# A two-block layer in f32r halves: head rows spread by one f32r matmul of two rows, embedding projection by split weights, rotary products in another order

## What is computed

```python
# first block
h = h + 0.5 * swiglu(rmsnorm(h, norm_ffn1), ffn1_w1, ffn1_w3, ffn1_w2)
z = rmsnorm(h, norm_mix) @ w_in
q, kc, vc, ksl, vsl, kw, vw, g, u = split(z)
q, kc, ksl, kw = rope(q), rope(kc), rope(ksl), rope(kw)     # x1*cos - x2*sin, x1*sin + x2*cos
o_nsa = nsa_attention(q, kc, vc, ksl, vsl, kw, vw, sigmoid(g), ...)
o_s5 = s5_mixer(u, ...)
h = h + concatenate([o_nsa, o_s5]) @ w_out
h = h + 0.5 * swiglu(rmsnorm(h, norm_ffn2), ffn2_w1, ffn2_w3, ffn2_w2)
h = h + sigmoid(rmsnorm(h, norm_ple) @ w_ple_gate) * (p @ w_ple)   # p: 512 x 256
h = rmsnorm(h, norm_final)
# second block, twice: projections, recurrence, and per head of the cell (4 heads of 256)
d = b[t] - b[s] + log_i[s]          # s <= t, b the running sum of log_f
m_t = max(m_inter, max(d)); w_intra = exp(d - m_t)
num = (q k^T * w_intra) v + ...; den = sum(q k^T * w_intra) + ...
h = num / max(|den|, exp(-m_t))
```

## Time and profile before

| | |
|---|---|
| median of 3 runs | 2105.43 us (2105.28 to 2106.63) |
| the profiled execution | 2098.56 us, its span 2096.8 us |
| TensorE busy | 1996.2 us, 95% of the span |
| VectorE, ScalarE, GpSimd busy | 1228.6, 844.0, 362.4 us |
| mean granted TensorE clock | 0.965 of full speed |

### The profile page before, as it was taken

One profiled execution on the slowest core, in us unless ns is written; L12 is line 12 of the kernel. 1 busy time (PEld: TensorE's weight loads), 2 busy tenths in 40 slices (PEclk: granted clock), 3 DMA queues, 4 the chain that ended last, 5 costly groups with the idle time before them and its releaser, 6 DMA issues.

```text
span 2096.8 us, 21907 instructions
## 1 busy us (share of the span) xinstructions
PE 1996.2 (95%) x8662; PEld 1526.7 (73%) x8662; DVE 1228.6 (59%) x1636; ACT 844.0 (40%) x1264; POOL 362.4 (17%) x319
## 2 busy tenths in 40 slices
PE   7999999988977899999999999999999899999997
PEld 5888888756533478888887777776788778766886
DVE  5764444677696446665665686924662559335742
ACT  5331323201456543322333347644542366445531
POOL 2000001156244010000001302601201024102002
PEclk9999999998778999999999999999999999999998
DMA  5332232221000134654652222321123222220221
GB/s 185 100 118 75 100 104 97 84 71 53 26 0 1 65 131 158 208 182 158 198 173 68 71 91 78 101 81 51 51 91 100 83 86 81 91 70 31 91 90 61
DMA packets 53174, 196.70 MB, mean 94 GB/s; under 512 B 5969, under 2 KB 6481, under 8 KB 52433
## 3 DMA queue, kind: packets, MB, share of 16 engines
q1 hardware_dynamic: 42912, 159.50, 22.7%
q0 software_dynamic: 7504, 28.58, 4.3%
q10 hardware_dynamic: 2656, 7.23, 1.0%
HBM read 192.14 MB, written 2.10 MB: 93 GB/s over the span
## 4 chain that ended last, share of the span: by engine, by line
PE 78%; DVE 13%; ACT 4%; POOL 2%; issue 1%; DMA 1%; ACTq 0%; POOLq 0%; DVEq 0%
PE PS L554 77%; DVE AR L1546 3%; DVE AR L1779 2%; DVE WLO L1543 2%; ACT WHI L1078 1%; DVE AR L2021 1%; DVE AR L1869 1%; PE PS L768 1%; DVE AR L1988 0%; DMA H<-in_xT 0%; POOL ACC L2137 0%; DVE ACC L1546 0%; DMA RAW<-in_w_out 0%; ACT SQ L1093 0%; DVE AR L1759 0%
## 5 line engine op out<-in xcount | busy, mean ns | idle before, releaser
L554 PE MATMUL PS<-HNH,WHI 128*128 128x512 f32 x1632 | 658.7, 404 | 15.8 <-ACT HNH L1109 13.9
L1543 DVE TENSOR_TENSOR WLO<-RAW,WHI 128x1024 fp32r<-128x1024 f32 (+1 forms) x270 | 371.6, 1379 | 514.7 <-ACT WHI L1078 514.5
L554 PE MATMUL PS<-HNH,WLO 128*128 128x512 f32 x1632 | 639.8, 392 | 3.4 <-DVE WLO L1543 3.4
L1078 ACT ACTIVATE WHI<-RAW 128x1024 fp32r<-128x1024 f32 (+1 forms) x270 | 295.9, 1096 | 687.0 <-PE PS L554 613.3
L554 PE MATMUL PS<-HNL,WHI 128*128 128x512 f32 x1632 | 436.0, 390 | 0.1
L554 PEld LDWEIGHTS PS<-HNH,WHI 128*128 128x128 f32 x1632 | 308.2, 189 | 96.4 <-issue 22.0
L554 PEld LDWEIGHTS PS<-HNH,WLO 128*128 128x128 f32 x1632 | 308.5, 189 | 77.9 <-issue 8.9
L554 PEld LDWEIGHTS PS<-HNL,WHI 128*128 128x128 f32 x1632 | 307.4, 188 | 64.8 <-DVE HNL L1546 1.0
L554 PE MATMUL PS<-AR 128*128 128x512 f32 (+12 forms) x700 | 213.3, 519 | 8.7 <-DVE SQ L1763 3.6
L2137 POOL TENSOR_TENSOR ACC<-ACC,SQ 128x512 f32<-128x512 f32 x46 | 62.7, 1362 | 782.2 <-ACT SQ L1093 781.3
L554 PEld LDWEIGHTS PS<-AR 128*128 128x128 f32 (+5 forms) x700 | 99.4, 199 | 90.2 <-issue 57.6
(11 more groups left out here) (299 smaller groups left out, 2421.6 us busy)
## 6 DMA issues: line engine op xcount, KB each, us to landing
RAW<-in_w_in SPq DMA_DIRECT2D x80, 512.0 KB, 3.5
AR<-in_w_ada POOLq DMA_DIRECT2D x48, 512.0 KB, 3.9
RAW<-in_w13a SPq DMA_DIRECT2D x44, 512.0 KB, 3.3
RAW<-in_w13b SPq DMA_DIRECT2D x44, 512.0 KB, 4.2
RAW<-in_w_out SPq DMA_DIRECT2D x40, 512.0 KB, 3.5
RAW<-in_w2a SPq DMA_DIRECT2D x16, 704.0 KB, 4.1
RAW<-in_w2b SPq DMA_DIRECT2D x16, 704.0 KB, 5.6
RAW<-in_w_inA SPq DMA_DIRECT2D x12, 512.0 KB, 3.3
```

Source lines behind the costliest of these rows:

```text
L554: return pe.matmul(o, l, r, start=start, stop=stop, skip_group_check=True)
L1078: act.activation(hi_of(name, i), raw_of(name, i), ACT.Copy).then_inc(*HI.up(name, i))
L1543: dve.tensor_tensor(lo_of(name, i), raw_of(name, i), f32(hi_of(name, i)), S_).then_inc(*LO.up(name, i))
```

## The change

- **Cell.** VectorE writes for each of NM and MM a pair of rows, a high row (rounded to f32r) at partition 32h and a low row at 32h + 1, with signs turned (`minus_rows`: one operation that writes the rounded row, one that forms both by the mask lo_row); sel_i and sel_f now put each head's gates on two partitions. TensorE opens a head with two f32r matmuls of two rows instead of two f32 matmuls of one. The ones that it multiplies with are copied once to f32r by ScalarE.
- **Embedding projection.** w_ple goes through the split stream as two tiles of 1024 columns, each for four output tiles, at m = 0 and m = 3; p is split once, ahead of the second feed-forward. ScalarE waits there for its load.
- **Rotary order.** GpSimd makes the cosine product in the step "rope". Turn 2 stands behind "positions" 0, the turns 4 and 5 come one step later, 6 and 7 within the value products.

The diff, with one line of context:

```diff
@@ -22,7 +22,7 @@
     ("norm_g", 16), ("b_ada", 48), ("rg_conv_w", 64), ("rg_conv_b", 16), ("rg_b_a", 16), ("rg_b_x", 16),
-    ("rg_lam", 16), ("ml_conv_w", 64), ("ml_conv_b", 16), ("ml_norm_g", 16), ("final_g", 8), ("b_if", 2),
+    ("rg_lam", 16), ("ml_conv_w", 64), ("ml_conv_b", 16), ("ml_norm_g", 16), ("final_g", 8), ("b_if", 2), ("lo_row", 1),
 ]
@@ -75,7 +75,9 @@
     ffn("b")
-    out.extend(("w_pg", m, 1024, True) for m in range(8))
+    for c, tiles in enumerate((range(3), range(3, 8))):
+        out.append(("w_ple", c, 1024, True))
+        out.extend(("w_pg", m, 1024, True) for m in tiles)
     for l in range(2):
@@ -223,19 +225,22 @@
             yield "pairs", 0
-        elif i > 2:
-            yield "turn", i - 1
         if i == 3:
...
             yield "pairs", 1
+        if i in (3, 4):
+            yield "turn", i - 1
+        if i > 5:
+            yield "turn", i - 2
         if i >= 4:
...
     yield "positions", 1
-    yield "turn", 7
     for z in range(2):
...
             yield "v", z, tt
+            if z == 0 and tt < 2:
+                yield "turn", 6 + tt
             yield from some(1)
@@ -336,6 +341,9 @@
         OH, OL = tiles_(place("OH", at_ar, 8 * T, F32R)), tiles_(place("OL", at_ar + 9216, 8 * T, F32R))
+        ROW_HALF = tiles_(place("ROW_HALF", at_ar + 4096 + T, T, F32R))[:, 0, :]
+        ROWS = tiles_(place("ROWS", at_ar + 4096 + 4 * T, 2 * T, F32R))
+        ONE = place("ONE", at_ar + 20640, P, F32R)
         MASK = place("MASK", at_ar + 20520, 2 * P, mybir.dt.bfloat16)
@@ -380,7 +388,7 @@
             loaded(f"x{k}")
-        for name in ("vecs", "consts", "s5_bc", "small_w", "pairs", "w_ple", "pT", "c", "rg_w", "w_if"):
+        for name in ("vecs", "consts", "s5_bc", "small_w", "pairs", "pT", "c", "rg_w", "w_if"):
             loaded(name)
@@ -491,8 +499,8 @@
 
-        WP = ar(0, 2, 1024)
         PT_ = ar(2048, 2, T)
+        PTH, PTL = tiles_(place("PTH", at_ar, 2 * T, F32R)), tiles_(place("PTL", at_ar + 2 * T, 2 * T, F32R))
         ACC2 = ar(3072, T)
@@ -826,18 +834,29 @@
 
+            ple_banks = {}
             for m in range(KD):
-                ps2, b2 = take(pe, "w_ple", m)
-                pe.wait_ge(*loaded("w_ple").at())
-                pe.wait_ge(*loaded("pT").at())
-                for k in range(2):
-                    t = mm(ps2[:, :], WP[:, k, P * m:P * m + P], PT_[:, k, :], k == 0, k == 1)
-                t.then_inc(*P_.up("w_ple", m))
+                if m in (0, 3):
+                    c = m // 3
+                    hi, lo = rows(hi_of("w_ple", c), T), rows(lo_of("w_ple", c), T)
+                    for j in range(4):
+                        w = slice(P * j, P * j + P)
+                        ple_banks[4 * c + j] = ps, b = take(pe, "ple", 4 * c + j)
+                        for k in range(2):
+                            pe.wait_ge(*HI.at("w_ple", c))
+                            pe.wait_ge(*A.at("pt", k))
+                            mm(ps[:, :], hi[:, k, w], PTH[:, k, :], k == 0, False)
+                            pe.wait_ge(*LO.at("w_ple", c))
+                            mm(ps[:, :], lo[:, k, w], PTH[:, k, :], False, False)
+                            pe.wait_ge(*V.at("pt", k))
+                            t = mm(ps[:, :], hi[:, k, w], PTL[:, k, :], False, k == 1)
+                        t.then_inc(*P_.up("ple", 4 * c + j))
+                    P_.name("w_ple", c)
                 b = tile("w_pg", m, HNHk, HNLk, hn("ple"))
...
                 give(b, V, "ple_in", m)
-                give(b2, V, "ple_out", m)
+                give(ple_banks[m][1], V, "ple_out", m)
             P_.name("ple_done")
@@ -1002,13 +1021,14 @@
                     if step == "open":
-                        r = slice(32 * h, 32 * h + 1)
+                        r = slice(32 * h, 32 * h + 2)
                         bm[h] = take(pe, "cell_m", l, h)
                         pe_, be = take(pe, "cell_e", l, h)
+                        pe.wait_ge(*A.at("one"))
                         pe.wait_ge(*V.at("nm", l))
-                        mm(bm[h][0][:, :], const("ones")[r, :], NM[r, :], True, True).then_inc(*P_.up("cell_m", l, h))
+                        mm(bm[h][0][:, :], ONE[r, :], ROWS[r, 1, :], True, True).then_inc(*P_.up("cell_m", l, h))
                         pe.wait_ge(*V.at("mm", l))
-                        mm(pe_[:, :], const("ones")[r, :], MM[r, :], True, True).then_inc(*P_.up("cell_e", l, h))
+                        mm(pe_[:, :], ONE[r, :], ROWS[r, 0, :], True, True).then_inc(*P_.up("cell_e", l, h))
                         give(be, A, "em", l, h)
@@ -1300,8 +1320,10 @@
             act.wait_ge(*P_.at("w_out", KD - 1))
-            act.dma_start(AR[:, 0:2048], D["w_ple"]).then_inc(*loaded("w_ple").up())
             act.dma_start(PT_, D["pT"]).then_inc(*loaded("pT").up())
+            for k in range(2):
+                act.wait_ge(*loaded("pT").at())
+                act.activation(PTH[:, k, :], PT_[:, k, :], ACT.Copy).then_inc(*A.up("pt", k))
             ffn("b")
@@ -1325,6 +1347,8 @@
                     rs_sqrt("ple")
+                if m in (0, 3):
+                    hi_next()
                 act.wait_ge(*V.at("ple_in", m))
@@ -1441,6 +1465,8 @@
 
+                if l == 0:
+                    act.activation(ONE[:, :], ONES, ACT.Copy).then_inc(*A.up("one"))
                 values(0)
@@ -1475,7 +1501,7 @@
                         act.wait_ge(*V.at("cell", l, h - 2, 1) if h > 1 else P_.at("qk2_done", l))
-                        act.activation(head_em(h), bank("cell_e", l, h)[:, :], ACT.Exp, scale=-1.0).then_inc(*A.up("em", l, h))
+                        act.activation(head_em(h), bank("cell_e", l, h)[:, :], ACT.Exp).then_inc(*A.up("em", l, h))
                     elif step == "score":
@@ -1909,17 +1935,24 @@
                 hnl("n2", "norm_ffn2", m)
+            for k in range(2):
+                dve.wait_ge(*A.at("pt", k))
+                dve.tensor_tensor(PTL[:, k, :], PT_[:, k, :], f32(PTH[:, k, :]), S_).then_inc(*V.up("pt", k))
             ffn("b")
...
                     rs("ple")
+                    lo_next()
                 q = m % 2
+                if m == 3:
+                    lo_next()
                 dve.wait_ge(*P_.at("w_pg", m))
...
                 dve.wait_ge(*A.at("ple", m))
-                dve.tensor_tensor(TMP[:, q, :], bank("w_ple", m)[:, :], TMP[:, q, :], M_).then_inc(*V.up("ple_out", m))
+                dve.wait_ge(*P_.at("ple", m))
+                dve.tensor_tensor(TMP[:, q, :], bank("ple", m)[:, :], TMP[:, q, :], M_).then_inc(*V.up("ple_out", m))
                 mine()
@@ -2048,9 +2081,19 @@
                 mine()
-                dve.tensor_scalar(NM, MM, -1.0, None, M_).then_inc(*V.up("nm", l))
+                lo_row = vec("lo_row")
+
+                def minus_rows(z, *name):
+
+                    dve.tensor_scalar(ROW_HALF, MM, 1.0, None, M_).then_inc(*V.up("row_half", l, z))
+                    mine()
+                    stt(ROWS[:, z, :], f32(ROW_HALF), lo_row, MM, M_, S_).then_inc(*V.up(*name))
+
+                minus_rows(1, "nm", l)
                 mine()
-                dve.tensor_tensor(MM, MM, FC, A_).then_inc(*V.up("mm", l))
+                dve.tensor_tensor(MM, MM, FC, A_).then_inc(*V.up("mm_f", l))
+                mine()
+                minus_rows(0, "mm", l)
                 lo_next(3)
@@ -2178,11 +2221,10 @@
                     pool.wait_ge(*loaded("consts").at())
+                    pool.tensor_tensor(ROPE_TO[i], TMP[:, i % 4, :], COS, M_).then_inc(*G.up("rope", i))
                 elif step == "turn":
...
                     dst = ROPE_TO[i]
-                    pool.wait_ge(*V.at("rope", i))
-                    pool.tensor_tensor(dst, TMP[:, i % 4, :], COS, M_).then_inc(*G.up("rope", i))
                     pool.wait_ge(*V.at("turn", i))
@@ -2322,7 +2364,7 @@
         for h in range(4):
-            s[4 * z + h::32, 32 * h] = 1.0
+            s[4 * z + h::32, 32 * h:32 * h + 2] = 1.0
         c[n] = s
@@ -2368,7 +2410,7 @@
     A["w_pg"] = _tiles(I["w_ple_gate"][0], P)
-    A["w_ple"] = _tiles(I["w_ple"][0], 1024)[0]
+    A["w_ple"] = _tiles(I["w_ple"][0], T)
     A["c"] = np.ascontiguousarray(I["c_2"].reshape(1024))
@@ -2399,6 +2441,7 @@
         "ml_norm_g": two(I["ml_norm_g_2"]), "final_g": _cols(I["final_g_2"]), "b_if": bif,
+        "lo_row": (np.arange(P) % 32 == 1).astype(f)[:, None],
     }
```

## The result

| | before | after |
|---|---|---|
| median, four runs each in one sitting | 2105.36 us | 2082.52 us (2081.93 to 2084.16) |
| ratio, 95% interval | | 0.9908 (0.9894 to 0.9922) |
| both once more in another sitting | 2100.35 us, 9 runs | 2085.60 us, 5 runs; ratio 0.9929 (0.9915 to 0.9942) |
| profiled execution | 2098.56 us | 2084.16 us, span 2082.4 |
| TensorE, VectorE busy | 1996.2, 1228.6 us | 1983.1, 1244.6 us |

The change is faster by 0.7 to 0.9%, 14.8 us in one sitting and 22.8 in the other. The forecast was 19.1 us, to 2086.3 us; its range of 2078 to 2098 holds both medians. One execution of the later kernel u_cell took 5177.42 us, the other four 2088.6 to 2094.6; it is in no ratio.

A forecast was written before the change was run, and what follows sets the result against it. TensorE was taken as the bound almost everywhere, except the first block's mixing stage, where VectorE waited for GpSimd's cosine product. Rotary 11.0, cell 8.1 and embedding 0 sum to 19.1 us: from 2105.43 to 2086.3 us, range 2078 to 2098.

The forecast's parts named there:

- the rotary term: Mixing stage of the first block: moving the cosine product and turns removes VectorE's waits, 15.8 us, for a gain of 11.0.
- I take 4.0 us instead of 2.95: First positions on VectorE, with GpSimd busy beside them: they end at 443.1, so the compression product starts 5.3 us sooner.
- the walk: Item-by-item count through the mixing stage with the rows' durations: VectorE ends 11.5 us ahead, less 0.5, gain 11.0.
- some 4.6 us of waiting in the place of 5.76: VectorE's low half behind turn 5: it waits for its weights instead of the turn, leaving VectorE 7.8 us ahead.
- ceiling of 14 us: Mixing stage: by the exclusive port lock, VectorE's and GpSimd's work adds up, so the gain could not pass about 14 us.
- Cell, forecast 8.1: Head openings: 1.26 us less for each of heads 1 to 3 in both layers, 7.6, plus 0.5 for head 0.
- Rival (b): Cell openings: two-row f32r products cost as much as f32, so only the rotary part gains, 2094.4 us; chance 0.06.
- Embedding, forecast 0: Gated embedding: TensorE saves 3.2 us but VectorE becomes the bound at about 6.05 a tile; gain 0.2, taken as 0.
- (a): Only the cell gains; the lock and weight loads give the rotary waits back whole, 2097.3 us; chance 0.15.
- (c): Mixing stage: TensorE stays at full clock from 434 to 505, up to 33 us less in all, 2073; chance 0.09.
- (e): Attention part: scan groups slide under GpSimd's work at 2.87 us each; with ten, 9.6 us slower, 2115; chance 0.06.

The follow-up runs named there:

- u_cell: The changed kernel with the cell's old openings, one f32 row per product and no row pairs: median 2089.23 us, ratio to the kernel before 0.9937.
- f_light: The changed kernel without five of GpSimd's six sums for the final norm in the gated embedding: 2083.92 us, one run.
- f_copypos: The changed kernel with plain one-input copies in place of the first position sums: 2085.60 us, one run.
- u_rotary: The changed kernel with the old rotary order, GpSimd's cosine product back in "turn": median 2090.82 us, ratio to the kernel before 0.9946.
- e_moves: The changed kernel with compression ahead of turns 6 and 7, an embedding low half after the last tile, cell halves behind head 0's first score: 2080.19 us.
- f_best: The changed kernel with e_moves' second and third moves, and the step "gated" of heads 2 and 3 behind score 3: 2072.82 us, ratio to before 0.987.

## Why the prediction was right, step by step

The total came out (forecast 2086.3, measured 2082.5 and 2085.6), by terms that missed in opposite directions. That it lies between the two sittings' gains is in part luck: the rotary term was half as large again as what was measured, and the 1.70 us of clock in the cell were not foreseen.

- **Rotary order, forecast 11.0, measured 7.3.** The mechanism held: no wait for the cosine product, and most of it given back. The size failed in two steps. The first is "I take 4.0 us instead of 2.95" for the positions: they took 5.32, so the compression product began 4.0 us sooner (447.59 - 3.05 against 448.50), not 5.3. The 1.3 us ran on. Behind the three scan groups VectorE was 0.8 ahead (forecast 1.5), behind turn 3's scans 1.6 (2.9), at the low half of 469.88 4.8 (6.6), behind the low half of 481.62 4.2 (7.8), at the second positions 7.3 (11.5). The second step is this low half: the walk gained 1.2 us there ("some 4.6 us of waiting in the place of 5.76"), the trace lost 0.6. It waited 5.59 us, two short waits for TensorE (0.24 and 0.17) came ahead of it, and it took 1.48 itself for 1.31. These two steps make 3.1 us of the 4.2 that are missing at the second positions. I had taken the positions' slowing as a third; with GpSimd busy all along it was 5.32 against about 2.0 without it (the second positions at 499.14 took 2.03).
- **The rule on the shared port.** I weighed it as a ceiling of 14 us. The Trainium skill (SBUF — State Buffer, section "SBUF: two separate sides") says that whichever of the two engines starts first keeps the pair for the whole instruction. f_light's row agrees almost to the letter: 0.55 us behind the end of GpSimd's sum for an operation of 0.69. The Trainium skill (SBUF — State Buffer, section "Who interferes with whom") counts copies and `tensor_scalar` among the operations that can take the shared pair; the 4.93 us of f_copypos agree, and I had not used it. An estimate by that rule, from rows: the positions would take their 2.03 us and the three products of GpSimd that the last three of the four sums met (442.72, 444.17, 445.72; alone such a one takes 1.27), 5.8 us against the measured 5.32 and my 4.0.
- **Cell, forecast 8.1, measured 9.1.** The opening is 0.65 us as forecast, heads 1 to 3 gain 1.24 each (1.26). Head 0 gains 0.05 in the first layer, not 0.26, with the wait of 0.98 us that stands in the place of the opening (forecast about 1). Rival (b), two rows as dear as f32, fell. What was missing from the sum is the 1.70 us of lower clock in the second layer, behind the long openings; I had read head 0 in the first layer alone.
- **Embedding, forecast 0, measured 0.** VectorE took 5.95 us a tile (forecast 6.05) and was the bound. ScalarE did wait for its load before the second feed-forward, 2.93 us, but that landed in 4.1 us, not 6.2, and the high half went at 777.50. The reciprocal behind it came at 783.48, before at 788.03, so that is 782.05 on the time axis of before, where I had 784.5. TensorE did not stand there:

```profile
776.45 1.15 ACT L1326 ACTIVATE PTH<-AR 128x512 fp32r<-128x512 f32 x2 [2.93 <-DMA AR<-in_pT]
777.50 1.04 ACT L1098 ACTIVATE WHI<-RAW 128x1024 fp32r<-128x1024 f32 x1
```

- **The rivals.** (a), the cell alone, fell with u_rotary. (c), full clock from 434 to 505, fell: 0.86 as before. (e), scans that slide under GpSimd in the attention part: all 128 scans took 71.6 us for 69.4, 2.2 us and not 28.7. Of them 80, 20 groups and not the 24 of the prediction, lie behind the second positions; these took 43.5 for 42.4. Its mechanism is real, though, ahead of the attention: it is what ate e_moves' first move and part of the rotary gain.
- **The sum.** By the traces 7.3 + 9.1 = 16.4 us, 2.7 less than forecast. The pair of profiled executions gives 14.4, since the changed one lost 3.05 at its start. The sittings gave 22.8 and 14.8; scatter of the size of the table's third column lies between, and what differed between the sittings is not explained further.

## What to carry to other kernels

An operation of VectorE with its inputs in SBUF that moves beside a busy GpSimd is priced by GpSimd's instructions that it meets, not by its own time with some added. In the mixing stage, where both engines together are the bound, 15.8 us of removed waits gave 7.3. A wait behind a removed one shows where the next gain is: the moves of f_best brought 8.2 us, more than the 7.3 of the rotary order. And when terms of some us are to be told apart, count between two operations of the trace that stand on either side of the edit: whole executions of this kernel scatter by as much.

## What was not expected of the hardware

- One-input f32 copies of VectorE from SBUF to SBUF took 4.93 us for four of 128x248 beside GpSimd, two-input sums 5.32; alone four sums take 2.0.
- f32 products of one row and of two take the same 1.91 us for two of 512 columns with weights, f32r ones of two rows 0.65.
- An f32 opening in place of an f32r one, 1.26 us longer, cost another 1.70 us through the clock in the product behind it (4.97 us for 3.27), in the second layer of three kernels out of three; in the first layer 3.27 stands in all of them. Why the second layer and not the first is open.
- The same code took 223.1, 225.0 or 226.5 us in one stretch of the second layer, with a granted clock of 1.00, 0.96 or 0.92 in the last 45 us of it, and TensorE's clock over equal busy time was 0.55 in one execution and 0.63 in another.
- The first meeting of VectorE and GpSimd in the run went one of two ways (a low half of 1.22 us or of 2.6 to 3.1), and the first reciprocal came 1.1 to 3.3 us later in the second way.
